# Turning three of the second layer's gelu chunks by DMA transposes instead of on TensorE, and multiplying them by the scan's state one unit later

## The chip, the core and the metric

One core of a Trainium2 chip runs the whole kernel. The metric is the time of one execution in microseconds (us). Before the change three runs gave 3112.25 us as their median, from 3112.09 to 3113.0.

## The reference, cut to what matters

The kernel computes three transformer-like blocks in a row on 256 tokens with 2048 features, in float32. The change lies in the second layer of the first block, the mixer with a recurrence:

```python
def rglru_mixer(h, w_in, conv_w, conv_b, gate_w, gate_b, lru_lambda, w_out):
    proj = h @ w_in
    y_branch, x_branch = jnp.split(proj, 2, axis=-1)
    y_branch = jax.nn.gelu(y_branch)
    xc = causal_depthwise_conv(x_branch, conv_w, conv_b)
    ...                                   # gates r, i from xc; a, u from them
    _, hs = lax.associative_scan(combine, (a, u), axis=1)
    return (hs.astype(h.dtype) * y_branch) @ w_out
```

y_branch is 256 tokens by 2048 features. Its 2048 columns are computed in four chunks of 512. A product has the tokens on the partitions; the scan runs along the tokens, so its state hs has the features on the partitions, and so must hs * y_branch, because it is the stationary side of the next product. So each gelu chunk has to be turned (transposed) before it is multiplied by hs.

## The kernel before, in words

**Units and chunks.** Weights are streamed from DRAM in units of 128 x 1024 float32 (512 KB, two tiles of 128 rows by 512 columns). A chunk is 512 output columns: eight units, and 8 x 12 products on TensorE. Each float32 weight is taken apart into a hi part (ScalarE, L701) and a lo part (VectorE, L1437), and TensorE makes three products per tile and token half (L2337 to L2339). The raw ring has six slots, the ring of hi and lo parts five.

**Order by hand.** Each engine has a class (`Sync`, `Scalar`, `Vector`, `Tensor`, `Pool`) and walks through the same model; in `chunk` a loop over j = 0 to 7 holds one conversion of a unit (`conv`) and, at given j, the side work of this chunk and of the chunk before (`prev`). The loop is written out by hand; nothing is planned by costs. ScalarE and VectorE convert unit j + 3 in their step j, so their step j lies some three units ahead of TensorE's unit j. Conversion of unit u into a ring of five needs TensorE to have finished unit u - 5. TensorE does units 0 and 1 first for token half 0 and then for token half 1, and units 6 and 7 likewise; the others for both halves at once.

**Handing a chunk over.** ScalarE reads token half 0 out of PSUM in its step 7, ahead of that step's conversion (`evac`, L732), and half 1 behind the loop. TensorE starts the next chunk only when half 0 is out (`pair_free`), and its half 1 only when half 1 is out. For a gelu chunk ScalarE then squares it (L739), VectorE makes the tanh's argument (L1456), ScalarE the tanh in step 0 of the next chunk (L747), VectorE the product (L1483). This leaves the gelu, with the tokens on the partitions, in `stg`.

**The recurrence beside it.** During the three chunks that follow the first gelu chunk, and during the first chunk of the product with odd_w_out, a quarter of the scan runs with each: VectorE's scans in steps 1 and 2 (L1918); ScalarE's decays in step 4, which wait for the scans (L1136, L1137, L1140); VectorE's ratio in step 5 (L1904), which waits for them; ScalarE's root in step 6 (L1144), which waits for the ratio; VectorE's drive in step 7 (L1912).

**The turn before the change.** TensorE transposes the eight 128 x 128 blocks of `stg` into PSUM (`turn`, L2368) ahead of its unit 4, VectorE multiplies them by `lru_h` in its step 4 (L1511), ScalarE writes the hi part in step 6 (L806), VectorE the lo part in step 6 (L1618). That instruction raises the semaphore split_done, which TensorE waits for ahead of its next turn. In the first chunk of the product with odd_w_out the turn stands ahead of unit 3.

**The other way to turn, used elsewhere in this kernel.** For 42 chunks of the other stages VectorE takes the upper and lower two bytes of `stg` apart into `tmp` (`bytes_part`, L1537, two copies), SyncE issues one DMA transpose of 2-byte elements (L536), and VectorE puts the bytes together again (`bytes_join`, L1553, two copies). Such a pending chunk has the kind "bytes". With width -1 the transposes go back into `stg` (turned_stg) and not into a buffer of their own. A chunk whose prev is of kind "bytes" waits on TensorE, ahead of its first unit, for all of split_done that is counted so far.

Of the kernel before, what the change touches and what calls it, by code (L numbers as in the profile page):

```python
# [31 lines left out]
ALU = mybir.AluOpType  # L32
# [8 lines left out]
CH = 512  # L41
# [217 lines left out]
def build(nc, i, out):  # L259
# [15 lines left out]
    with ExitStack() as ctx:  # L275
# [148 lines left out]
        class Program:  # L424
# [24 lines left out]
            setup = params = chunk = gates = s5_params = glu = final = mix_at = heads_at = prepare = nothing  # L449

            def turn_slot(self, prev, units, kind):
                if prev is None or prev.kind == "flip" or prev.kind == "bytes" and prev.to[0] != "conv":
                    return -1
                if prev.to[0] == "conv":
                    return 3 if prev.kind == "bytes" else 2
                return 4 if prev.kind == "rope" or prev.kind == "gelu" == kind else min(3, units - 2)
# [21 lines left out]
        class Sync(Program):  # L478
# [61 lines left out]
            def chunk(self, kind, w, units=8, width=CH, lead=None, slot=None, prep=None, order=None,  # L540
                      n=0, apart=False, params=False, **_):
                src, t0, col0 = w
                if lead and lead.kind == "post":
                    self.T.add("x_ready", len(TILES))
                cols = slice(col0, col0 + width) if isinstance(col0, int) else bass.ds(col0, width)
                for j in range(units):
                    if self.preloaded:
                        self.preloaded -= 1
                        continue
                    each = UNIT // width  # L550
                    k = each * (order[j] if order else j)
                    tiles = slice(t0 + k, t0 + k + each) if isinstance(t0, int) else bass.ds(t0 + k, each)
                    self.unit(src[:, tiles, cols], width)
                    if j == 1 and self.apart[0] is not None:
                        self.bytes_turn(self.apart[0])
                        if params:
                            self.load_b_raw()
                    if prep is not None:
                        self.prepare(prep, j)
                    if slot is not None:  # L560
                        self.mix_at(slot + j)
                self.apart = self.apart[1], n if apart else None
# [102 lines left out]
        class Scalar(Program):  # L665
# [144 lines left out]
            def chunk(self, kind, w, units=8, width=CH, prev=None, lead=None, to=None, dst=None, n=0, ss=True,  # L810
# [11 lines left out]
                else:  # L822
                    at = self.turn_slot(prev, units, kind)
                    for j in range(units - AHEAD + 1 if tail else units):
                        if j == units - 1 and kind != "flip":
                            if lead:
                                self.root(D)
                                self.eng.wait_ge(sems["rs_ready"], T.add("rs_ready"))
                            self.evac(kind, ps, 0, dst, width)
                        self.conv()  # L830
                        for p, what, at_j in parts:
                            if at_j == j and what == "square":
                                self.part_square(p)
                            if at_j == j and what == "split":
                                self.late_hi(xlead, p, True)
                        if prep is not None:
                            self.prepare(prep, j)
                            if tail and j == 4:
                                self.prepare(prep, 6)
                        if slot is not None:  # L840
                            self.mix_at(slot + j)
                        if slot1 is not None:
                            self.heads_at(slot1 + j)
                        if order and j >= WINDOW_AT:
                            self.split_window(j - WINDOW_AT)
                        if j == (0 if units == 4 else 1) and self.unsquared is not None:
                            self.square_sums(self.unsquared)
                            self.unsquared = None
                        if j == 0 and final and n:
                            self.part_square(n - 1)  # L850
                        if j == (4 if units == 8 else 1) and stage is not None and n < NCH - 1:
                            for k in ((0, 1) if n == 0 else (n + 1,)):
                                name, l = STAGES[stage]
                                self.load_gain(4 * stage + k, i[name][l, k * CH:(k + 1) * CH])
                        if j == 3 and final and n < NCH - 1:
                            for k in ((0, 1) if n == 0 else (n + 1,)):
                                self.load_gain(16 + k, i["final_g_2"][k * CH:(k + 1) * CH])
                        if prev and prev.kind == "bytes":
                            if j == 3:
                                if prev.width >= 0:  # L860
                                    self.bytes_hi(prev)
                                elif prev.to[0] == "conv":
                                    self.bytes_conv(prev)
                                else:
                                    T.add("split_done")
                                self.stg_till = T.at("split_done")
                        elif j == at:
                            self.split(prev.to)
                        if j == 0 and prev and prev.kind == "flip":
                            self.flip_read(prev)  # L870
                        if j == 3 and prev and prev.kind == "flip":
                            self.flip_hi(prev)
                        if prev and (prev.to[0], j) in (("conv", at + 3), ("lru", at + 2)):
                            self.split_conv(prev.to)
                        if j == 0 and prev and prev.kind == "gelu":
                            self.gelu_finish()
                        if j == 2 and constant:
                            self.lru_constant()
                        if j in (1, 2) and gate is not None:
                            self.gate(gate, j - 1)  # L880
                        if j == 4 and lru is not None:
                            self.lru_decay(lru)
                        if j == 6 and lru is not None:
                            self.lru_root(lru)
# [523 lines left out]
        class Vector(Program):  # L1408
# [93 lines left out]
            def split(self, to):  # L1502
# [4 lines left out]
                    return self.conv_tap(to[1], 0, turn_ps)  # L1507
                if to[0] == "lru":
                    self.eng.wait_ge(sems["turned"], T.at("turned"))
                    self.eng.wait_ge(sems["lru_scanned"], to[1] // 4 + 1)  # L1510
                    nc.vector.tensor_tensor(conv_o[:], turn_ps[:], lru_h[:, to[1]:to[1] + 4], ALU.mult  # L1511
                                            ).then_inc(sems["lru_z"], 1)
                    T.add("lru_z")
                    T.add("split_done")
                    return
                if to[0] in ("plain", "halves"):
                    T.add("split_done")
# [4 lines left out]
                else:  # L1522
                    self.eng.wait_ge(sems["split_hi"], T.add("split_hi"))
                    a = nc.vector.tensor_tensor(to[1], turn_ps[:], to[0].bitcast(F32), ALU.subtract)
                a.then_inc(sems["split_done"], 1)
                T.add("split_done")

            def bytes_part(self):
# [12 lines left out]
            def bytes_join(self, prev):  # L1541
# [5 lines left out]
                if own:  # L1547
                    to = stg[:].rearrange("p m n -> p (m n)").rearrange("p (k s) -> p k s", k=4)
                else:
                    to = joined if prev.to[0] == "conv" else prev.to[1]  # L1550
                to = to.bitcast(U16).rearrange("p k (m t two) -> p m k t two", m=M, two=2)
                for half in range(2):
                    a = nc.vector.tensor_copy(to[:, :, :, :, half],  # L1553
                                              src[:, 8 * half:8 * half + 8].rearrange("p (m k) t -> p m k t", m=M))
                told = "joined" if own or prev.to[0] == "conv" else "split_done"
                a.then_inc(sems[told], 1)
                T.add(told)

# [62 lines left out]
            def chunk(self, kind, w, units=8, width=CH, prev=None, lead=None, to=None, dst=None, n=0, ss=True,  # L1621
# [11 lines left out]
                else:  # L1633
                    at = self.turn_slot(prev, units, kind)
                    for j in range(units - AHEAD + 1 if tail else units):
# [17 lines left out]
                        if j == (0 if units == 4 else 3) and stage is not None and n:  # L1653
                            self.apply_gain(n - 1)
                        if prev and prev.kind == "bytes":
                            if j == 0:
                                self.bytes_part()
                            if j == 3:
                                self.bytes_join(prev)
                            if j == 4 and prev.width >= 0:  # L1660
                                self.bytes_lo(prev)
                            if j == 3 and prev.to[0] == "conv":
# [8 lines left out]
                            self.split_conv(prev.to)  # L1671
                        if prev and prev.to[0] == "lru" and j in (1, 2):
                            self.lru_scan(prev.to[1] // 4, j - 1)
                        if j == 0 and prev and prev.kind == "gelu":
                            self.gelu_finish()
                        if j == 2 and constant:
                            self.lru_constant()
# [1434 lines left out]
        def model(e):  # L3112
# [31 lines left out]
                if c:  # L3144
                    e.gates(c - 1)
            for c in range(4):
                prev = e.chunk("gelu", (w_odd_in, 0, c * CH), x=XT, prev=prev, to=("lru", 4 * c),
                               gate=c + 2 if c < 2 else None, lru=c)
                if c == 0:
                    e.gates(3)  # L3150
# [89 lines left out]
```

## Time and profile before

| | us |
|---|---|
| three runs, median | 3112.25 |
| the profiled execution | 3112.18 |
| its span in the trace | 3110.4 |
| PE busy | 3097.9 (100%) |
| DVE busy | 1989.5 (64%) |
| ACT busy | 1557.4 (50%) |
| POOL busy | 265.6 (9%) |

PE is TensorE's products, PEld its weight loads, DVE is VectorE, ACT ScalarE, POOL GpSimd. The profiled execution lies 0.07 us from the median of the runs, and 1.78 us of it lie outside the span. A busy PE in this table means that its products overlap without a gap; a matmul of 512 columns is shown with some 0.39 us, and the next one starts 0.23 us after it.

### The profile page before, as it was taken

How to read it: one execution, taken by the hardware profiler on the slowest of the kernel's cores; microseconds unless marked ns; L12 is line 12 of the kernel's file. 1: busy time of each engine (PE TensorE's matmuls, PEld its weight loads, DVE VectorE, ACT ScalarE, POOL GpSimd, SP SyncE). 2: the span in 40 equal slices, each digit the busy share in tenths (PEclk: the TensorE clock that was granted, in tenths of full speed). 3: DMA queues.
4: the chain of work that ended last, by engine and by line, in shares of the span. 5: the costliest groups of instructions: out<-in, count | busy, mean ns of one | idle time of the engine just before them, and what ended most of it. 6: DMA issues, size and time to landing. Idle time of an engine off the chain costs nothing.

```text
span 3110.4 us, 37341 instructions
## 1 busy us (share of the span) xinstructions
PE 3097.9 (100%) x14652; PEld 2570.7 (83%) x14652; DVE 1989.5 (64%) x2290; ACT 1557.4 (50%) x2157; POOL 265.6 (9%) x330
## 2 busy tenths in 40 slices
PE   9999999999999999999999999999999999999999
PEld 8788888888888888888888888888888888888887
DVE  6787765656565768676665655668885555555455
ACT  6666543434444669554443434564455443444344
POOL 0000000000000020011820007820000000000000
PEclk9999999999999999999999999999999999999999
DMA  7655676767667556666675766767655766666674
GB/s 246 169 163 172 189 220 193 217 199 205 208 201 225 171 181 190 212 195 212 195 221 184 221 200 223 250 219 228 198 156 176 213 201 202 200 200 209 190 210 155
DMA packets 416944, 623.64 MB, mean 201 GB/s; under 512 B 121169, under 2 KB 132865, under 8 KB 416769
## 3 DMA queue, kind: packets, MB, share of 16 engines
q1 hardware_dynamic: 411376, 614.62, 64.3%
q10 hardware_dynamic: 5392, 6.64, 0.7%
q8 instruction: 116, 1.90, 0.2%
q14 instruction: 60, 0.48, 0.0%
HBM read 587.09 MB, written 11.01 MB: 192 GB/s over the span
## 4 chain that ended last, share of the span: by engine, by line
PE 95%; DVE 2%; ACT 2%; issue 1%; DMA 0%; SPq 0%; ACTq 0%
PE pair L2337 31%; PE pair L2339 30%; PE pair L2338 30%; DVE lo L1437 1%; PE turn_ps L2368 1%; ACT hi L701 0%; PE pair L2768 0%; PE misc_ps L2674 0%; DVE xt_hl L1795 0%; DMA raw<-in_even_w_in 0%; PE misc_ps L2688 0%; DMA turned_bytes<-tmp 0%; PE pair L2657 0%; PE pair L2659 0%; PE pair L2658 0%
## 5 line engine op out<-in xcount | busy, mean ns | idle before, releaser
L1437 DVE TENSOR_TENSOR lo<-raw,hi 128x1024 fp32r<-128x1024 f32 x1084 | 1337.9, 1247 | 711.5 <-ACT hi L701 699.0
L701 ACT ACTIVATE hi<-raw 128x1024 fp32r<-128x1024 f32 x1084 | 1128.9, 1057 | 867.7 <-PE pair L2339 855.5
L2337 PE MATMUL pair<-hi,xt_hl 128*128 128x512 f32 (+1 forms) x2780 | 1089.6, 392 | 2.6 <-DVE lo L1437 1.3
L2339 PE MATMUL pair<-lo,xt_hl 128*128 128x512 f32 (+1 forms) x2780 | 1079.5, 388 | 0.0
L2338 PE MATMUL pair<-hi,xt_hl 128*128 128x512 f32 (+1 forms) x2780 | 1078.8, 388 | 0.0
L2337 PEld LDWEIGHTS pair<-hi,xt_hl 128*128 128x128 f32 x2780 | 522.1, 188 | 114.5 <-issue 2.5
L2339 PEld LDWEIGHTS pair<-lo,xt_hl 128*128 128x128 f32 x2780 | 521.9, 188 | 108.7
L2338 PEld LDWEIGHTS pair<-hi,xt_hl 128*128 128x128 f32 x2780 | 522.4, 188 | 103.6
L2337 PE MATMUL pair<-hi,ht_h 128*128 128x512 f32 x1504 | 586.4, 390 | 0.1
L2339 PE MATMUL pair<-lo,ht_h 128*128 128x512 f32 x1504 | 585.2, 389 | 0.0
L2338 PE MATMUL pair<-hi,ht_l 128*128 128x512 f32 x1504 | 585.2, 389 | 0.0
L2337 PEld LDWEIGHTS pair<-hi,ht_h 128*128 128x128 f32 x1504 | 282.3, 188 | 58.8 <-DVE ht_l L1563 0.5
L2339 PEld LDWEIGHTS pair<-lo,ht_h 128*128 128x128 f32 x1504 | 282.3, 188 | 58.5
L2338 PEld LDWEIGHTS pair<-hi,ht_l 128*128 128x128 f32 x1504 | 282.4, 188 | 58.3
L921 ACT ACTIVATE ht_h<-stg 128x1024 fp32r<-128x1024 f32 x38 | 40.3, 1061 | 157.4 <-DVE stg L1553 157.4
L732 ACT ACTIVATE stg<-pair 128x512 f32<-128x512 f32 x64 | 38.3, 598 | 149.8 <-PE pair L2339 149.1
L2872 POOL TENSOR_TENSOR lru_h<-ht_h,ht_l 128x1024 f32<-128x1024 f32 x4 | 9.8, 2438 | 1164.7 <-ACT gate_i L1120 1164.7
L732 ACT ACTIVATE stg<-pair,stat 128x512 f32<-128x512 f32 x62 | 42.5, 685 | 95.4 <-PE pair L2339 94.9
L1553 DVE COPY stg<-turned_bytes 128x1024 uint16<-128x1024 uint16 x76 | 53.7, 762 | 52.7 <-DMA turned_bytes<-tmp 52.5
L1473 DVE SCALAR_TENSOR_TENSOR acc<-pair,stat,acc 128x512 f32<-128x512 f32 x48 | 36.0, 750 | 75.2 <-PE pair L2339 75.2
L1477 DVE TENSOR_TENSOR xres<-pair,xres 128x512 f32<-128x512 f32 x39 | 26.9, 690 | 55.4 <-PE pair L2339 55.4
L1537 DVE COPY tmp<-stg 128x1024 uint16<-128x1024 uint16 x84 | 54.4, 690 | 0.0
(344 smaller groups left out, 1700.0 us busy)
## 6 DMA issues: line engine op xcount, KB each, us to landing
raw<-in_mlp_w SPq DMA_DIRECT2D x512, 512.0 KB, 4.4
raw<-in_w_gate SPq DMA_DIRECT2D x88, 512.0 KB, 4.4
raw<-in_w_up SPq DMA_DIRECT2D x88, 512.0 KB, 4.0
raw<-in_w_down SPq DMA_DIRECT2D x88, 512.0 KB, 4.4
raw<-in_even_w_in SPq DMA_DIRECT2D x68, 512.0 KB, 4.4
raw<-in_odd_w_in SPq DMA_DIRECT2D x64, 512.0 KB, 4.0
raw<-in_w_in SPq DMA_DIRECT2D x64, 512.0 KB, 4.6
raw<-in_even_w_out SPq DMA_DIRECT2D x32, 512.0 KB, 4.1
```

The source lines that it names most:

```text
L701: nc.scalar.activation(hi[:, r], raw[:, slot], ACT.Copy).then_inc(sems["hi_ready"], 1)
L732: a = nc.scalar.activation(to, ps[:, m, 0:width], func, scale=scale)
L921: nc.scalar.activation(prev.to[0], stg[:].rearrange("p m (f s) -> p (m f) s", s=SEQ), ACT.Copy).then_inc(sems["split_hi"], 1)
L1437: nc.vector.tensor_tensor(lo[:, r], raw[:, slot], hi[:, r].bitcast(F32), ALU.subtract).then_inc(sems["lo_ready"], 1)
L1473: a = nc.vector.scalar_tensor_tensor(dst[:, m], ps[:, m], st(RS2 + m), dst[:, m], ALU.mult, ALU.add)
L1477: a = nc.vector.tensor_tensor(dst[:, m], ps[:, m], dst[:, m], ALU.add)
L1537: a = nc.vector.tensor_copy(planes[:, half], halves[:, half])
L1553: a = nc.vector.tensor_copy(to[:, :, :, :, half], src[:, 8 * half:8 * half + 8].rearrange("p (m k) t -> p m k t", m=M))
L2337: nc.tensor.matmul(to, xh[:, t0 + k, tok], h[:, k], start=s, stop=False)
L2338: nc.tensor.matmul(to, xl[:, t0 + k, tok], h[:, k], start=False, stop=False)
L2339: mm = nc.tensor.matmul(to, xh[:, t0 + k, tok], l[:, k], start=False, stop=e)
L2368: a = nc.tensor.transpose(turn_ps[:, k, m * P:(m + 1) * P], stg[:, m, k * P:(k + 1) * P], ident[:])
```

## The change

The first three gelu chunks get `apart`, so they are handed on as "bytes", with n = -3. In the chunk behind such a one:

- VectorE: the bytes are taken apart in step 1 (ahead of the scans of that step), put together in `tmp` in step 5, and multiplied by the scan's state right behind it, in step 5, ahead of the ratio. The lo part moves from step 6 to step 7.
- SyncE issues the DMA transpose behind unit 2 of its chunk, from `tmp` into `stg`.
- ScalarE waits in step 6 for the joined bytes, ahead of the root; the hi part moves from step 6 to step 7, behind the evacuation of half 0 and that step's conversion.
- TensorE: eight transposes less; the count of split_done goes up ahead of unit 4 without a turn.

The fourth gelu chunk is turned on TensorE as before.

```diff
             def turn_slot(self, prev, units, kind):
-                if prev is None or prev.kind == "flip" or prev.kind == "bytes" and prev.to[0] != "conv":
+                if prev is None or prev.kind == "flip" or prev.kind == "bytes" and prev.to[0] not in ("conv", "lru"):
                     return -1
+                if prev.kind == "bytes" and prev.to[0] == "lru":
+                    return 5
@@ Sync.chunk
-                    if j == 1 and self.apart[0] is not None:
+                    if self.apart[0] is not None and j == (2 if self.apart[0] == -3 else 1):
                         self.bytes_turn(self.apart[0])
@@ Scalar.chunk
                         if prev and prev.kind == "bytes":
-                            if j == 3:
+                            if j == (6 if prev.to[0] == "lru" else 3):
...
+                                elif prev.to[0] == "lru":
+                                    T.add("split_done")
+                                    self.eng.wait_ge(sems["joined"], T.add("joined"))
@@ Vector
+            def lru_z(self, t0, src):
+                T = self.T
+                self.eng.wait_ge(sems["lru_scanned"], t0 // 4 + 1)
+                self.eng.wait_ge(sems["joined"], T.at("joined"))
+                nc.vector.tensor_tensor(conv_o[:], src, lru_h[:, t0:t0 + 4], ALU.mult).then_inc(sems["lru_z"], 1)
+                T.add("lru_z")
+                T.add("split_done")
...
                         if prev and prev.kind == "bytes":
-                            if j == 0:
+                            if j == (prev.to[0] == "lru"):
                                 self.bytes_part()
-                            if j == 3:
+                            if j == (5 if prev.width < -1 else 3):
                                 self.bytes_join(prev)
+                            if j == 5 and prev.to[0] == "lru":
+                                self.lru_z(prev.to[1], joined)
@@ model
             for c in range(4):
-                prev = e.chunk("gelu", (w_odd_in, 0, c * CH), x=XT, prev=prev, to=("lru", 4 * c),
+                prev = e.chunk("gelu", (w_odd_in, 0, c * CH), x=XT, prev=prev, to=("lru", 4 * c), n=-3, apart=c < 3,
                                gate=c + 2 if c < 2 else None, lru=c)
```

In ScalarE's and VectorE's loops the moved steps stand at `at + 2`, with `at` from turn_slot: 4 + 2 before, 5 + 2 after.

## Rows read from the trace of the kernel before

**Rows 1.** The page: busy time by engine, and the chain that ended last.

```profile
PE 3097.9 (100%) x14652; PEld 2570.7 (83%) x14652; DVE 1989.5 (64%) x2290; ACT 1557.4 (50%) x2157; POOL 265.6 (9%) x330
...
PE 95%; DVE 2%; ACT 2%; issue 1%; DMA 0%; SPq 0%; ACTq 0%
```

**Rows 2.** The stretch of the second gelu chunk: busy us by engine, clock, DMA.

```profile
core 0: us, PE busy (x) PEld busy (x) DVE busy (x) ACT busy (x) POOL busy (x), PEclk, DMA share, GB/s
...
1170.00:1197.00 27.00, 27.00 (x141) 22.90 (x139) 25.10 (x20) 26.82 (x37) 5.19 (x2) 1.00 0.61 194
```

**Rows 3.** Timeline of PE, second gelu chunk: start, us, engine, line, operation, count.

```profile
1179.70 0.39 PE L2337 MATMUL pair<-hi,xt_hl 128*128 128x512 f32 x1
...
1185.14 1.03 PE L2368 MATMUL turn_ps<-ident,stg 128*128 128x128 f32 x8
1185.93 0.48 PE L2337 MATMUL pair<-hi,xt_hl 128*128 128x512 f32 x1
1186.25 0.40 PE L2338 MATMUL pair<-hi,xt_hl 128*128 128x512 f32 x1
```

**Rows 4.** The chain that ended last, 1188 to 1198 us: start, us, what.

```profile
1191.14 1.99 ACT hi L701 x2
1193.13 0.94 ACT ht_h L806
...
1195.39 1.16 ACT lru_s L1144
1196.55 0.58 ACT stg L732
1197.17 0.50 PE pair L2337
```

**Rows 5.** Timeline of ACT, third gelu chunk; in brackets idle time before and its releaser.

```profile
1208.97 0.51 ACT L1136 ACTIVATE lru_a<-gate_r,c_lru 128x256 f32<-128x256 f32 x1 [2.12 <-DVE lru_h L1918]
...
1213.28 1.99 ACT L701 ACTIVATE hi<-raw 128x1024 fp32r<-128x1024 f32 x2
1215.17 1.04 ACT L806 ACTIVATE ht_h<-conv_o 128x1024 fp32r<-128x1024 f32 x1
...
1218.59 0.67 ACT L732 ACTIVATE stg<-pair,stat 128x512 f32<-128x512 f32 x1
...
1240.84 0.67 ACT L732 ACTIVATE stg<-pair,stat 128x512 f32<-128x512 f32 x1
```

**Rows 6.** Timeline of DVE, the same chunk.

```profile
1205.37 1.27 DVE L1918 TENSOR_TENSOR_SCAN lru_h<-lru_a,lru_s 128x256 f32<-128x256 f32 x2
...
1211.11 1.22 DVE L1511 TENSOR_TENSOR conv_o<-turn_ps,lru_h 128x1024 f32<-128x1024 f32 x1
1214.36 1.22 DVE L1437 TENSOR_TENSOR lo<-raw,hi 128x1024 fp32r<-128x1024 f32 x1 [2.03 <-ACT hi L701]
1215.50 1.22 DVE L1904 SCALAR_TENSOR_TENSOR lru_s<-lru_s,gate_r 128x1024 f32<-128x1024 f32 x1
```

**Rows 7.** Timeline of DVE, a chunk of the first MLP that is turned by DMA.

```profile
362.34 1.29 DVE L1537 COPY tmp<-stg 128x1024 uint16<-128x1024 uint16 x2
363.55 3.71 DVE L1437 TENSOR_TENSOR lo<-raw,hi 128x1024 fp32r<-128x1024 f32 x3
369.27 1.39 DVE L1553 COPY stg<-turned_bytes 128x1024 uint16<-128x1024 uint16 x2 [2.02 <-DMA turned_bytes<-tmp]
```

**Rows 8.** DMA issues by line: kind, count, median us from issue to landing.

```profile
turned_bytes<-tmp SPq DMA_TRANSPOSE x38, 5.0
...
stg<-tmp SPq DMA_TRANSPOSE x4, 3.8
```

**Rows 9.** Timeline of PE: its last product.

```profile
3102.69 0.39 PE L2339 MATMUL pair<-lo,ht_h 128*128 128x512 f32 x1
```

**Rows 10.** Stretches at the end of the span (columns of rows 2).

```profile
3107.50:3108.00 0.50, 0.00 (x0) 0.00 (x0) 0.00 (x0) 0.00 (x0) 0.00 (x0) 0.99 1.04 401
3108.00:3108.50 0.50, 0.00 (x0) 0.00 (x0) 0.00 (x0) 0.00 (x0) 0.00 (x0) 0.50 1.04 397
```

More of the change, by code:

```diff
@@ L863, in chunk @@
                                     self.bytes_conv(prev)
+                                elif prev.to[0] == "lru":
+                                    T.add("split_done")
+                                    self.eng.wait_ge(sems["joined"], T.add("joined"))
                                 else:
                                     T.add("split_done")
-                                self.stg_till = T.at("split_done")
+                                if prev.to[0] != "lru":
+                                    self.stg_till = T.at("split_done")
                         elif j == at:
@@ L874, in chunk @@
                             self.split_conv(prev.to)
-                        if j == 0 and prev and prev.kind == "gelu":
+                        if j == 0 and prev and (prev.kind == "gelu" or prev.kind == "bytes" and prev.to[0] == "lru"):
                             self.gelu_finish()
@@ L1509, in split @@
                     self.eng.wait_ge(sems["turned"], T.at("turned"))
[L1510 to L1514, printed above, removed]
+                    self.lru_z(to[1], turn_ps[:])
                     return
@@ L1549, in bytes_join @@
                 else:
-                    to = joined if prev.to[0] == "conv" else prev.to[1]
+                    to = joined if prev.to[0] in ("conv", "lru") else prev.to[1]
                 to = to.bitcast(U16).rearrange("p k (m t two) -> p m k t two", m=M, two=2)
@@ L1554, in bytes_join @@
                                               src[:, 8 * half:8 * half + 8].rearrange("p (m k) t -> p m k t", m=M))
-                told = "joined" if own or prev.to[0] == "conv" else "split_done"
+                told = "joined" if own or prev.to[0] in ("conv", "lru") else "split_done"
                 a.then_inc(sems[told], 1)
@@ L1673, in chunk @@
                             self.lru_scan(prev.to[1] // 4, j - 1)
-                        if j == 0 and prev and prev.kind == "gelu":
+                        if j == 0 and prev and (prev.kind == "gelu" or prev.kind == "bytes" and prev.to[0] == "lru"):
                             self.gelu_finish()
```

## The prediction, written before the result was known

> **What bounds the kernel now.** I read the page's busy table and chain first [rows 1]: TensorE is busy for 3097.9 of 3110.4 us and holds 95% of the chain. So what is taken off TensorE shortens the kernel, and what makes it wait lengthens it; work of other engines costs nothing until then. The averages of 64% and 50% for VectorE and ScalarE don't hold in the stage of the change: in the 27 us of the second gelu chunk ScalarE is busy for 26.82 and VectorE for 25.10 [rows 2]. The third view, the chain cut to this place [rows 4], is the one that decides: it doesn't run over TensorE there but over ScalarE: conversions, the hi part (L806), the root (L1144), the evacuation (L732), and only then TensorE's next chunk at 1197.17. TensorE ends the chunk before at 1185.14 + 0.88 + 48 x 0.2267 = 1196.9 (the two figures are worked out in the next part, [rows 3]), so it already starts 0.27 us late. Every us put into this chain shows in the time.
>
> I call the gelu chunks G0 to G3 and the first chunk of the product with odd_w_out W0. The side work of G0 runs beside G1, that of G1 beside G2, and so on. By "evac" I mean ScalarE's evacuation of token half 0, in its step 7.
>
> **What goes.** From the start of the eight transposes to the first product behind them 0.79 us pass, and that product is followed after 0.32 instead of 0.23 [rows 3]: a turn costs 0.88 us. Three turns: -2.64. The 24 products between 1179.70 and 1185.14 give 0.2267 each [rows 3], so a chunk without a turn takes 96 x 0.2267 = 21.76 us on TensorE.
>
> **What comes in, on VectorE.** Taking the bytes apart holds it for 363.55 - 362.34 = 1.21 us, joining them for some 1.4 [rows 7]. The first stands in step 1 ahead of that step's scans, so the scans end 1.2 us later. ScalarE's decays wait for these scans, with 2.12 us of idle time in front of them [rows 5], so they start 1.2 later as well, and so does all that follows. The join comes in step 5, behind a conversion that itself waits for ScalarE (2.03 us [rows 6]). Before, the product with the state (L1511) was done in step 4, inside that waiting time and thus free; now it stands behind the join, ahead of the ratio (L1904), for which ScalarE's root waits.
>
> The lengthening of the stretch from ScalarE's conversion of step 5 to its evac: before it is 1218.59 - 1213.28 = 5.31 [rows 5]. Now: ScalarE's conversion till VectorE's starts 1.12, that 1.14 (1214.36 to 1215.50 [rows 6]), join 1.5 with the semaphore behind it, product 1.13, ratio 1.21, root 1.16 less 0.1 of overlap (its start to the evac's [rows 4]), 0.07 of signal: 7.23. That is +1.92. The moved hi part (L806) leaves this stretch, where it hides nothing any more, and comes behind the evac.
>
> **What comes in, on TensorE.** A chunk whose prev is "bytes" waits ahead of its first unit for all split_done so far. For G2 and G3 that includes the lo part of the chunk before (L1618), now in step 7: evac 0.57, conversion 0.97, hi part 1.04, signal, VectorE behind its own conversion, lo part 1.22: 4.1 us from the start of evac to TensorE's start. Before, only the evac counted (0.6).
>
> **The sum, step by step.** G1: TensorE would be done at 1196.9 - 0.88 = 1196.0. ScalarE's conversion of step 5 stays at 1191.14 [rows 4], because behind the gate work of this chunk the decays didn't wait for the scans; evac at 1191.14 + 7.23 = 1198.4; G2 starts at 1198.4 + 4.1 = 1202.5. Stall 6.5.
> G2: a period from evac to evac was 1240.84 - 1218.59 = 22.25 [rows 5]. Now it grows by 1.24 (bytes apart, ahead of the scans), 1.92 (above) and 0.97 to 1.0 (hi part between the evacuations of half 0 and half 1, from which the next gelu hangs; in its old place it was beside the chain): 26.4 us. Evac at 1224.8, G3 could start at 1228.9; TensorE is done with G2 at 1202.5 + 21.8 = 1224.3. Stall 4.6.
> G3: evac at 1224.8 + 26.4 = 1251.2. W0 isn't preceded by a "bytes" chunk and waits for the evac only, until 1251.9; TensorE done at 1250.6. Stall 1.3.
> W0: its units 6 and 7 need G3's lo part, which hangs from the evac of G3; the turn is back. Against TensorE the chain is 1.1 us later than before, where it had 0.4 to spare, and the hi part of G2's work costs it 0.5 more: stall 1.3.
> Stalls 6.5 + 4.6 + 1.3 + 1.3 = 13.7, less 0.27 of the stall that stands there now, less 2.64: +10.8 us. The same laying-out of steps over the kernel before gives the evacs 1218.61 and 1240.82, where the rows have 1218.59 and 1240.84 [rows 5], so the arithmetic of the chain is good to a tenth; the risk lies in the order that I read from the code.
>
> **What is moved and costs nothing.** SyncE: three transposes, each behind unit 2's load. It waits there for the bytes to be apart; behind it stand only loads of units five and more ahead, some 13 us of cover. Issue to landing took 3.8 us into `stg` (4 of them) and 5.0 into buffers of their own (38) [rows 8]. From the bytes apart to the join there are 10 us in G2 and 12 in G1: hidden. If landing took over 10 us, the rest would come onto the period; 12 us give +14.7 in all. The nearest rows have joins that waited 2.02 us when only three conversions lay between [rows 7]. ScalarE's wait for the join in step 6 ends before the ratio does, so it adds nothing. Copies bounded from both sides: join 1.39 [rows 7] to 2 us, each 0.1 us more shows three times. Nothing is gained by the moves but the transposes.
>
> **The clock.** All of this stage is granted full speed. After its last product, which starts at 3102.69 and ends at 3103.08, TensorE idles and the clock falls from 2.4 to 1.2 GHz at 3108.0, 4.9 us later [rows 9, 10]. The first stall of 6.5 us is longer than that, the second of 4.6 (3.1 if the first units of G2 are slow) isn't. I take it that the clock falls once. How long it stays low no row shows; bounds: nothing lost, and the first two units of G2 at half speed, 5.4 us lost. I take 2.5. Of a loss in G2 the first 1.5 us are hidden, for TensorE waits at the end of G2 for the chain anyway; but then the ring holds the conversions of G2 back. It leaves +1.0. Sum: +11.8.
> The Trainium skill ("TensorE: Matmul & The Clock Gate", section "HAM oscillation — how this bites in real kernels") says that an idle TensorE falls back to half rate, and that the work behind each such gap then starts cold, again and again. By that page the gap at G3 could be paid as well, which is a rival below; the end of this trace agrees with the rule as far as one fall goes.
>
> **Forecast.** The profiled execution took 3112.18 and stands 0.07 from the median. 3112.2 + 11.8 = 3124.0 us. Its own range, with join and signals 0.2 us off per chunk and the clock from 0 to 2.5: 3121 to 3127.
>
> **Rivals.**
> *Hidden after all (slower no more).* VectorE and ScalarE work ahead of TensorE, and the rings of five and six could swallow the delay. The place is evac against the end of TensorE's chunk, the price is 2.64 us gained: 3109.6. It decides if evac comes at most 21.2 us after TensorE's start. For it: TensorE's busy share of 100% in the table. Against it: that margin is used up already [rows 4], and 4.25 us go into each period. 7%.
> *Only the first stall counts*: what is late in G2 and G3 is caught up, since ScalarE's wait of 2.12 and VectorE's of 2.03 [rows 5, 6] shrink. -2.64 + 6.5 = +3.9: 3116.1. Against it: these waits are for one another, not spare. 6%.
> *The clock falls at both gaps and stays low for long* (two units at half speed behind each): +14.7 with one, +18.7 with both: 3127 to 3131. For it: rows 10; against it: the second gap is short. 6%.
> *The change gains* (the turns go and a wait in front of W0 goes too): under 3106 nothing in the rows would give. 1%.
>
> **How the numbers follow.** Forecast 80%, hidden 7, first stall only 6, clock 6, gain 1. A difference of 0.2% (6.2 us) is about what a measurement of this kernel can tell from none. Slower by more: 80 + 6 = 86%; within: 7 + 6 = 13%; faster: 1%. The range from 3117 to 3130 leaves out the first rival, the second by 1 us and the end of the third.
>
> **What would show it.** In the trace after: 24 transposes fewer at L2368; gaps on PE of some 6.5, 4.6 and 1.3 us at the starts of G2, G3 and W0, the first two released by VectorE's lo part and the third by ScalarE's evac; evac to evac 26.4 us instead of 22.25; the joins not waiting for the DMA; a granted clock under 1.00 in G2's first us. I am wrong if evac stays within 21.2 us of TensorE's start, if TensorE's start of G2 isn't released by the lo part, or if the joins wait for the transposes.

## The result, and the profile after

The changed kernel takes 3128.22 us (median of six runs, 3127.32 to 3129.1); the kernel before took 3112.28 in six. The ratio is 1.0051 with an interval of 1.004 to 1.0061: slower by 15.9 us. 3124.0 was forecast, with a range of 3117 to 3130. The time lies inside that range, but above the forecast's own 3121 to 3127, and inside the 3127 to 3131 of the rival in which the clock falls at both gaps; the part on why the prediction was right takes this up.

The page of the kernel after: busy time, the costliest products with what ended the idle time before them, and the transposes by line.

```profile
PE 3100.7 (99%) x14628; PEld 2571.2 (82%) x14628; DVE 1997.1 (64%) x2302; ACT 1557.3 (50%) x2157; POOL 265.6 (8%) x330
...
L2350 PE MATMUL pair<-hi,xt_hl 128*128 128x512 f32 (+1 forms) x2780 | 1091.6, 393 | 14.3 <-DVE ht_l L1629 11.9
...
L2381 PE MATMUL turn_ps<-ident,stg x148: 270/272/273, 39.1 to 3062.4; 128*128 128x128 f32 x148
```

24 transposes are gone (172 to 148), and TensorE is not less busy but more, by 2.8 us [rows 1]: the products run longer at a lower clock. The new idle time lies in front of products that wait for the lo part (L1629, which was L1618 before). Line numbers in this section are those of the changed kernel from here on; each experiment has those of its own kernel, a few lines off.

The timeline of PE: last product of G1 and first of G2, last of G2 and first of G3, first of W0, and W0's first one of units 6 and 7. Then PE's waits between 1170 and 1290 us (total, times, longest).

```profile
1196.16 0.39 PE L2352 MATMUL pair<-lo,xt_hl 128*128 128x512 f32 x1
1204.11 0.79 PE L2350 MATMUL pair<-hi,xt_hl 128*128 128x512 f32 x1 [7.56 <-DVE ht_l L1629]
...
1227.23 0.39 PE L2352 MATMUL pair<-lo,xt_hl 128*128 128x512 f32 x1
1231.92 0.79 PE L2350 MATMUL pair<-hi,xt_hl 128*128 128x512 f32 x1 [4.30 <-DVE ht_l L1629]
...
1257.75 0.50 PE L2350 MATMUL pair<-hi,ht_h 128*128 128x512 f32 x1 [0.95 <-ACT stg L734]
...
1276.17 0.50 PE L2350 MATMUL pair<-hi,ht_h 128*128 128x512 f32 x1 [0.89 <-DVE ht_l L1629]
```

```profile
PE pair L2350 <- DVE ht_l L1629: 12.7, 3, 7.6
...
PE pair L2350 <- ACT stg L734: 1.0, 1, 1.0
```

These are the stalls at G2, G3 and W0 with the releasers that were forecast; the third wait for the lo part (0.89) is W0's, ahead of its units 6 and 7, and was forecast too. Before the change G2 started at 1197.17 [rows 4]. A product that starts at 1227.23 frees its place 0.23 us later, so the true stalls are some 7.7, 4.5, 1.1 and 1.0 us.

The timeline of ACT in the kernel after, side work of G1 beside it, and the evacuations of the next two chunks:

```profile
1191.56 1.99 ACT L703 ACTIVATE hi<-raw 128x1024 fp32r<-128x1024 f32 x2
1197.70 1.28 ACT L1150 ACT_TABLE_LOAD   x1 [4.15 <-DVE lru_s L1917]
1198.99 1.15 ACT L1150 ACTIVATE lru_s<-lru_s,stat 128x1024 f32<-128x1024 f32 x1
1200.05 0.67 ACT L734 ACTIVATE stg<-pair,stat 128x512 f32<-128x512 f32 x1
1200.62 1.04 ACT L703 ACTIVATE hi<-raw 128x1024 fp32r<-128x1024 f32 x1
1201.56 1.04 ACT L808 ACTIVATE ht_h<-conv_o 128x1024 fp32r<-128x1024 f32 x1
...
1227.86 0.67 ACT L734 ACTIVATE stg<-pair,stat 128x512 f32<-128x512 f32 x1
...
1257.02 0.67 ACT L734 ACTIVATE stg<-pair,stat 128x512 f32<-128x512 f32 x1
```

And DVE in the same kernel and place:

```profile
1192.64 1.23 DVE L1443 TENSOR_TENSOR lo<-raw,hi 128x1024 fp32r<-128x1024 f32 x1 [1.03 <-ACT hi L703]
1193.78 1.38 DVE L1564 COPY tmp<-stg 128x1024 uint16<-128x1024 uint16 x2
1195.26 1.22 DVE L1535 TENSOR_TENSOR conv_o<-tmp,lru_h 128x1024 f32<-128x1024 f32 x1
1196.41 1.22 DVE L1917 SCALAR_TENSOR_TENSOR lru_s<-lru_s,gate_r 128x1024 f32<-128x1024 f32 x1
...
1201.69 1.22 DVE L1443 TENSOR_TENSOR lo<-raw,hi 128x1024 fp32r<-128x1024 f32 x1 [2.94 <-ACT hi L703]
1202.84 1.22 DVE L1629 SCALAR_TENSOR_TENSOR ht_l<-conv_o,ht_h 128x1024 fp32r<-128x1024 f32 x1
```

The same load in the kernel before, beside G2, and all four of these loads in the kernel after (busy time, mean ns, idle time before them):

```profile
1216.24 1.28 ACT L1144 ACT_TABLE_LOAD   x1
```

```profile
L1150 ACT ACT_TABLE_LOAD x4 | 5.1, 1283 | 12.5 <-DVE lru_s L1917 12.4
```

Read them together. The join (1193.78) has no bracket, so it does not wait for the DMA. From ScalarE's conversion of step 5 (1191.56) to its evac (1200.05) 8.49 us pass, where 5.31 passed before [rows 5]; I had 7.23. The missing 1.26 is in the second line of ACT's timeline: ScalarE's table load for the root, 1.28 us, starts only when the ratio is done (1197.63), so it lies on the chain. Before the change it started at 1216.24, ahead of the end of its ratio at 1216.72 [rows 6], and with no idle time in front of it. Of the four loads in the kernel after, three have 4.15, 4.15 and 4.14 us of idle time in front, together all of the 12.4; the fourth, beside W0, has no wait for a join ahead of it and does not wait. From evac to evac it is 27.81 us and then 29.16, where it was 22.25 [rows 5]. TensorE's start at 1204.11 follows 4.06 us behind the evac, as worked out (4.1).

The clock of the kernel after in the two gaps and behind them (columns of rows 2):

```profile
1200.00:1200.50 0.50, 0.00 (x0) 0.00 (x0) 0.00 (x0) 0.50 (x2) 0.00 (x0) 0.88 0.90 131
1200.50:1201.00 0.50, 0.00 (x0) 0.00 (x0) 0.00 (x0) 0.50 (x2) 0.00 (x0) 0.50 0.69 262
...
1230.50:1231.00 0.50, 0.00 (x0) 0.00 (x0) 0.50 (x2) 0.50 (x1) 0.00 (x0) 1.00 0.00 0
1231.00:1231.50 0.50, 0.00 (x0) 0.00 (x0) 0.50 (x1) 0.47 (x1) 0.00 (x0) 0.59 0.00 0
...
1231.50:1237.50 6.00, 5.58 (x13) 4.42 (x14) 5.84 (x6) 4.82 (x5) 0.00 (x0) 0.50 0.45 132
```

It fell from 2.4 to 1.2 GHz in both gaps, 3.8 and 3.5 us after the last product had ended. G2 took 1227.46 - 1204.11 = 23.35 us instead of 21.76, so 1.6 were lost; G3, measured in the same way, some 24.7, so 3.0.

The first evacuation of W0's product by DVE closes the stage, before and after:

```profile
1262.83 0.69 DVE L1475 COPY acc<-pair 128x512 f32<-128x512 f32 x1 [2.19 <-PE pair L2339]
```

```profile
1279.22 0.69 DVE L1481 COPY acc<-pair 128x512 f32<-128x512 f32 x1 [1.97 <-PE pair L2352]
```

It comes 16.39 us later, 0.42 of which are there already when the stage begins (ScalarE's 1191.14 [rows 4] against 1191.56). So 15.97 us of the 16.8 between the two spans lie in this stage; the profiled execution took 3129.1 us, 0.9 more than the median. TensorE's own account of the stage closes: stalls of 7.7 + 4.5 + 1.1 + 1.0, clock losses of 1.6 + 3.0, less the 0.3 of stall that stood there before, less 2.6 for the turns, make 16.0.

### The profile page after: what moved, and what is told of

The parts are those of the page before. It is cut to its first block, busy times and chain, and to the rows that moved or that the text cites. A ratio compares the mean times of both kernels' runs of the same rounds, so it can differ in the third digit from the quotient of the medians.

```text
span 3127.2 us, 37314 instructions
## 1 busy us (share of the span) xinstructions
PE 3100.7 (99%) x14628; PEld 2571.2 (82%) x14628; DVE 1997.1 (64%) x2302; ACT 1557.3 (50%) x2157; POOL 265.6 (8%) x330
## 4 chain that ended last, share of the span: by engine, by line
PE 57%; DVE 1%; ACT 1%; issue 0%; DVEq 0%; ACTq 0%
PE pair L2350 19%; PE pair L2352 18%; PE pair L2351 18%; DVE lo L1443 1%; PE pair L2781 0%; PE turn_ps L2381 0%; ACT hi L703 0%; PE misc_ps L2797 0%; DVE xt_hl L1808 0%; PE turn_ps L2840 0%; PE misc_ps L2802 0%; PE pair L2734 0%; DVE xres L1834 0%; DVE glu_z L2216 0%; PE misc_ps L2816 0%
## 5 line engine op out<-in xcount | busy, mean ns | idle before, releaser
L2350 PEld LDWEIGHTS pair<-hi,xt_hl 128*128 128x128 f32 x2780 | 523.2, 188 | 127.3 <-DVE ht_l L1629 12.7
```

The source lines that it names most:

```text
L2350: nc.tensor.matmul(to, xh[:, t0 + k, tok], h[:, k], start=s, stop=False)
```

## The experiments

All are against the kernel before on the same chip. The prediction's +10.8 us for chain and turns, with three table loads of 1.28 added, comes to +14.6; the stage measured 15.97, so some 1.3 are left for the clock. The following runs take links out of the chain, single ones at first.

**e1: the moves alone, without the DMA.** Edit to the kernel before:

```diff
-                return 4 if prev.kind == "rope" or prev.kind == "gelu" == kind else min(3, units - 2)
+                return 5 if prev.kind == "gelu" == kind else 4 if prev.kind == "rope" else min(3, units - 2)
```

> The kernel before with the steps moved and nothing else: the three gelu chunks are still turned on TensorE, now ahead of unit 5, multiplied in VectorE's step 5 ahead of the ratio, hi and lo part in step 7. No bytes, no DMA, no wait ahead of a chunk. Theory (the chain from ScalarE's evacuation to its next one bounds this stage, and every us that is put into it shows): product 1.14 ahead of the ratio, hi part 0.97 between the two evacuations, less what the hi part freed: period 23.6 us instead of 22.25, stalls of some 0.6, 1.0, 1.0 and 1.3 us, in all +3.8 us, 3116.1. Rival (only the bytes' copies, the wait ahead of the chunk and the clock cost anything): within 1 us of before, 3112 to 3113.

Measured: 3114.98 us against 3112.21, +2.8 (ratio 1.001, 1.0001 to 1.002). Evacs at

```profile
1196.74 0.66 ACT L732 ACTIVATE stg<-pair,stat 128x512 f32<-128x512 f32 x1
...
1220.17 0.66 ACT L732 ACTIVATE stg<-pair,stat 128x512 f32<-128x512 f32 x1
...
1243.59 0.67 ACT L732 ACTIVATE stg<-pair,stat 128x512 f32<-128x512 f32 x1
```

so 23.4 us apart, and TensorE waited for three of them (1.3 us in all) and once for the lo part (0.9). The same transposes, one step later and ahead of the ratio, already cost 2.8 us. The rival, that only bytes, wait and clock cost anything, falls. The forecast was 1 us too high.

**e2: ScalarE's wait for the join moved behind the root.** Edit to the changed kernel:

```diff
@@ Scalar.chunk, step 6
                                     T.add("split_done")
-                                    self.eng.wait_ge(sems["joined"], T.add("joined"))
@@ ahead of the evacuation
+                        if j == units - 1 and prev and prev.kind == "bytes" and prev.to[0] == "lru":
+                            self.eng.wait_ge(sems["joined"], T.add("joined"))
                         if j == units - 1 and kind != "flip":
```

> The changed kernel with ScalarE's wait for the joined bytes moved from step 6 (ahead of the root) to step 7 (ahead of the evacuation). Theory: with two waits in front of the root its table load of 1.28 us comes behind both; with one it is done while ScalarE waits, as before the change. Evac to evac 26.5 instead of 27.8 in the third gelu chunk, TensorE starts G2 at 1202.5 to 1202.9 instead of 1204.1; in all +11 us over before instead of +16, 3123 to 3124. Rival (the table load waits for the ratio's data whatever stands ahead of it): no difference, 3128.

Measured: 3124.56 us against 3112.21, +12.4 (1.0041, 1.0026 to 1.0056): 3.6 less than the changed kernel, where three loads of 1.28 are 3.84, and 0.6 above the forecast's upper end of 3124. ACT's timeline in e2:

```profile
1192.99 1.28 ACT L1151 ACT_TABLE_LOAD   x1
1197.09 1.15 ACT L1151 ACTIVATE lru_s<-lru_s,stat 128x1024 f32<-128x1024 f32 x1 [2.81 <-DVE lru_s L1918]
1198.14 0.67 ACT L734 ACTIVATE stg<-pair,stat 128x512 f32<-128x512 f32 x1
```

The load is back ahead of the wait, and the evac comes 7.16 us behind the conversion at 1190.98, where 7.23 had been worked out before the result. So it is the second wait that put the load behind. The clock fell at both gaps in e2 too: the second gap, 2.97 us long, cost TensorE some 1.7 us, which the forecast doesn't name. The Trainium skill ("Perfetto Trace Analysis", section "Identifying Dependency Chains") says that an instruction that waits for several engines may get semaphore instructions of their own ahead of it. That is near this case but not it, since both waits here are for VectorE (the join and the ratio); how the two waits were laid out as instructions no view here shows.

**e3: no wait ahead of G2 and G3.** Edit to the changed kernel:

```diff
-                if prev and prev.kind == "bytes":
+                if prev and prev.kind == "bytes" and prev.to[0] != "lru":
                     self.eng.wait_ge(sems["split_done"], T.at("split_done"))
+                if prev and prev.kind == "gelu" and kind == "set":
+                    self.eng.wait_ge(sems["split_done"], T.at("split_done", 1))
```

> The changed kernel without TensorE's wait for split_done ahead of G2 and G3 (they don't read what it guards); W0 waits for it instead. Theory (the chain of ScalarE and VectorE is the bound, the wait only moves the stalls): evac to evac stays near 27.7, stalls of 4.3, 4.3 to 5.9 and 4.3 to 5.9 us at G2, G3 and W0 instead of 7.6, 4.3 and 1.0, in all +14.6 over before, 3127, the 1.5 us less than the changed kernel being the clock's. Rival (the wait is the cause): only evac is late, the stalls ahead of G2 and G3 shrink by 3.4 us each, 3121.

Measured: 3127.83 us against 3112.21, +15.6 (1.005, 1.0035 to 1.0065). PE's timeline in e3, the starts of G2, G3 and W0:

```profile
1200.40 0.79 PE L2350 MATMUL pair<-hi,xt_hl 128*128 128x512 f32 x1 [4.21 <-ACT stg L734]
...
1227.87 0.50 PE L2350 MATMUL pair<-hi,xt_hl 128*128 128x512 f32 x1 [2.82 <-ACT stg L734]
...
1255.39 0.76 PE L2350 MATMUL pair<-hi,ht_h 128*128 128x512 f32 x1 [5.42 <-issue]
```

This is the run that says most. The wait that the trace of the changed kernel names for 12.7 us is gone, and 0.4 us come back. TensorE starts G2 3.7 us earlier and loses that further on: it waits 5.4 us ahead of W0, where it waited 0.95 and 0.89. The trace names no releaser for this last wait, and the edit puts a wait for split_done there; but W0 starts 0.77 us behind the evac at 1254.62, as it did in the changed kernel (0.73), so it is the evac that holds it and not the moved wait. The period (evacs at 1199.68, 1227.15 and 1254.62, 27.47 apart) is set by ScalarE and VectorE.

**e4: filler products in the gaps.** Edit to the changed kernel, ahead of the wait for split_done at G2 and G3; the products go to turn_ps and are not read:

```diff
+                if prev and prev.kind == "bytes" and prev.to[0] == "lru" and prev.to[1] >= 4:
+                    self.fill(24 if prev.to[1] == 4 else 16)
```

> The changed kernel with 24 products ahead of TensorE's wait at G2 and 16 ahead of that at G3, written to the free turn_ps and not read: the clock stays at full speed, and 2 to 2.5 us of each wait are left. It measures what the clock costs. Theory: evac of G3 comes 1.5 us earlier, since the conversions that wait for the first slow units of G3 aren't late: +14.6 over before, 3126.7. Rival (each us at half speed shows in full, 1.6 in G2 and 2.9 in G3): 4.5 less, 3123.7. Other rival (nothing): 3128.2.

Measured: 3127.22 us against 3112.21, +15.0 (1.0049, 1.0034 to 1.0064). At G3 the clock stayed at 1.00, and the period up to G3's evac is 1254.83 - 1227.35 = 27.48 instead of 29.16: 1.7 us of the 3.0 lost in G3 had shown. At G2 it fell all the same (below), so this run takes away only one of the two falls. It is 1.0 us faster than the changed kernel by the medians, and 1.5 by the stage in the two traces; the rest of what the clock took from TensorE is hidden in its waits for the chain.

**e5: the ratio ahead of the join.** Of e2, and in VectorE's step 5:

```diff
+                        if j == 5 and prev and prev.kind == "bytes" and prev.to[0] == "lru":
+                            self.lru_ratio(lru)
                         if prev and prev.kind == "bytes":
...
-                        if j == 5 and lru is not None:
+                        if j == 5 and lru is not None and not (prev.kind == "bytes" and prev.to[0] == "lru"):
                             self.lru_ratio(lru)
```

> Of e2 (join wait in step 7), and VectorE's ratio ahead of the join and the product in step 5. Theory: what stands between ScalarE's conversion of step 5 and its evac shrinks by 2.6 us of join and product, so evac of G1 comes at 1196.4 as in the kernel before; the period stays 24.5 us, by the bytes taken apart ahead of the scans (1.24) and the hi part between the evacuations (0.97). The wait for split_done is the only large one left: stalls of 4.6, 2.8 and 0.6 us, in all +5.2 over before, 3117.4. If the clock falls in the first gap, up to 1 us more. Rival (the join and the product themselves are too much for VectorE in this stage, wherever they stand): 3122 and more, as e2.

Measured: 3119.67 us against 3112.35, +7.3 (1.0024, 1.0015 to 1.0033), from 3118.13 to 3123.01. It takes 4.9 us less than e2, so join and product cost by their place, not by being there. It is 2.1 us over the forecast, and 1.1 over that with a fallen clock. PE and ACT in e5:

```profile
1201.08 0.80 PE L2353 MATMUL pair<-hi,xt_hl 128*128 128x512 f32 x1 [4.50 <-DVE ht_l L1630]
```

```profile
1196.33 0.69 ACT L734 ACTIVATE stg<-pair,stat 128x512 f32<-128x512 f32 x1 [0.16 <-DVE tmp L1565]
...
1223.30 0.69 ACT L734 ACTIVATE stg<-pair,stat 128x512 f32<-128x512 f32 x1 [1.02 <-PE pair L2355]
```

The first gap is the forecast one (4.6); the one at G3 is shorter, 1.5 instead of 2.8. The clock fell behind the first, and G2 took 24.7 us on TensorE. With the chain shorter, TensorE is late enough that the evac of G2 waits for it (1.02 us) and comes 26.97 us behind the evac of G1 instead of the 24.5 of the forecast. So here most of the 2.9 us lost show, where e4 found them half hidden.

**e6: e5, without the wait ahead of G2 and G3, and the bytes taken apart behind the scans.** The edit of e3 is in it, and SyncE's transpose stands behind unit 3; VectorE's part:

```diff
-                            if j == (prev.to[0] == "lru"):
+                            if j == 0 and prev.to[0] != "lru":
                                 self.bytes_part()
...
                             self.lru_scan(prev.to[1] // 4, j - 1)
+                            if j == 2 and prev.kind == "bytes":
+                                self.bytes_part()
```

> Of e5, and besides no wait for split_done ahead of G2 and G3 (as e3), and the bytes taken apart behind the scans of step 2 instead of ahead of those of step 1 (SyncE's transpose one unit later). Theory: period 23.3 us; stalls of 0.7, 1.2, 1.2 and 1.3 us and some 0.3 at unit 1 of each chunk, in all +2.7 over before, 3114.9: each of the two is worth what it puts into the chain. Rival (the chain isn't it, but the stalls at the starts of chunks, so without the wait the transposes' 2.6 us are gained): 3110.

Measured: 3114.97 us against 3112.35, +2.6 (1.0008, 0.9999 to 1.0017). As the theory has it (2.7); the rival's 3110 is missed by 5 us. Evacs come at 1196.38, 1219.44 and 1242.50, 23.06 apart (23.3 forecast). Two things were changed at once, so the run doesn't show what each is worth by itself.

**e7: e6, with the hi and the lo part of the products that are made beside G1 and G2 in steps 2 and 3 of the next chunk.** In ScalarE's loop (VectorE's alike, with step 3 and without the wait):

```diff
-                            self.split_conv(prev.to)
+                            if prev.kind == "bytes" and prev.to[0] == "lru" and prev.to[1] < 8:
+                                self.owed = prev.to
+                                self.eng.wait_ge(sems["lru_z"], T.at("lru_z", -1))
+                            else:
+                                self.split_conv(prev.to)
+                        if j == 2 and self.owed:
+                            self.split_conv(self.owed)
+                            self.owed = None
```

> Of e6, and the hi and the lo part of G1's and G2's products in steps 2 and 3 of the chunk behind, where ScalarE waits for TensorE. Theory: period 22.1 us as before the change, in all +0.4 over before, 3112.6: even with all put aside the transposes' 2.64 us are not gained, because ScalarE's and VectorE's chain of 22.1 us, not TensorE's 21.8, sets the period, and W0 waits 1.3 us for its last part. Rival (TensorE's time is what counts once the stalls are gone): 3109.6 to 3110.5.

Measured: 3112.64 us against 3112.35, +0.3 (1.0001, 0.9992 to 1.0011). Evacs at 1195.87, 1217.82 and 1239.75, 21.9 apart. Two waits are left on TensorE, 0.58 us for the lo part of a conversion in G1 (1191.17) and 0.99 for G3's lo part ahead of W0's units 6 and 7. The period is only 0.2 us over TensorE's 21.76, and the evac of G3 comes 1.09 us earlier than in the kernel before (1239.75 against 1240.84, 0.14 of it there when the stage begins); W0's wait gives that back. TensorE has 2.64 us less to do, and the two other engines don't let it gain by that.

**e8: only the first gelu chunk by DMA.** Edit to the changed kernel: `apart=c == 0`.

> The changed kernel with only the first of the gelu chunks turned by DMA (side work beside G1), the other two on TensorE as before. Theory: evac of G1 at 1199.7; G2's prev isn't of kind bytes, so TensorE waits for the evac alone: 4.3 us ahead of G2, 0.6 ahead of G3, nothing at W0, less one turn of 0.88: +3.8 over before, 3116.1, up to 3117.1 if the clock falls. Rival (each such chunk costs the same third of the loss): +5.3, 3117.6.

Measured: 3117.13 us against 3112.35, +4.8 (1.0015, 1.0005 to 1.0025), from 3116.4 to 3118.1. The gap at G2 is 4.21 us, released by the evac, and the clock falls behind it. This is the forecast with a fallen clock (3117.1) and near the rival's 3117.6, so by its time alone the run doesn't part the two. What speaks for the theory is the releaser and the length of the gap, and that TensorE waits nowhere else in the stage.

**e9 and e10: the ratio ahead of step 5's conversion,** in e7 and in the kernel before:

```diff
                             self.evac(kind, ps, 0, dst, width)
+                        if j == 5 and lru is not None:
+                            self.lru_ratio(lru)
                         self.conv()
```

> Of e7, and VectorE's ratio ahead of that step's conversion instead of behind it, so that ScalarE's root doesn't wait for a conversion of ScalarE, then of VectorE, then the ratio. Theory: the period of ScalarE and VectorE falls from 22.1 to 21.2 us, under TensorE's 21.8; only then can the turns' 2.64 us be gained, less 0.36 for W0's last part: 2.3 under before, 3110.0. Rival (W0's wait or something later gives it back): 3112.

> The kernel before with VectorE's ratio ahead of step 5's conversion, and nothing else. Theory: ScalarE's chain gets shorter, but TensorE with its turns (22.6 us a chunk) is the bound there; only the 0.27 us ahead of G2 can go: 0.1 to 0.3 under before, 3112.1. Rival (what e9 gains is the early ratio and not the turns): as much as e9.

Measured: e9 3110.86 us (3110.21 to 3112.33, 11 runs) against 3112.37 (21 runs), -1.5; the ratio 0.9996 has an interval of 0.9987 to 1.0005, so a gain is likely but not shown. e10 3112.23 (0.9999, 0.999 to 1.0008). ACT's evacs of G2 and G3 and DVE's first of W0 in e9:

```profile
1217.07 0.67 ACT L736 ACTIVATE stg<-pair,stat 128x512 f32<-128x512 f32 x1
...
1238.56 0.67 ACT L736 ACTIVATE stg<-pair,stat 128x512 f32<-128x512 f32 x1
```

```profile
1260.75 0.69 DVE L1491 COPY acc<-pair 128x512 f32<-128x512 f32 x1 [1.97 <-PE pair L2370]
```

The period is 21.5 us, under TensorE's 21.76, and the stage closes 2.08 us earlier than before; 0.46 of that is there already when it begins (evac of G0 at 1168.43 against 1168.89), so the stage itself gives 1.6 us of the forecast's 2.3. The early ratio in the kernel before brings nothing that can be told: there TensorE is the bound with its turns.

## Why the prediction was right, and where it was short

- *The chain through ScalarE bounds this stage.* Right for the changed kernel, and shown: e3 takes away the wait that the trace names and gets 0.4 us back, e2, e5, e6 and e7 shorten the chain and get back about what they take out. In the kernel before the chain was only close to the bound: a chunk with its turn takes TensorE 22.6 us, the period was 22.25, and e10 shortens the chain and gains nothing that can be told.
- *The turns give 2.64 us.* Right as a term of TensorE's time, but it is given back as a wait in every variant until the chain is under 21.8 us (e9; in e7 the period is 21.9 and nothing is gained).
- *Stalls of 6.5, 4.6, 1.3 and 1.3 us.* Measured 7.7, 4.5, 1.1 and 1.0. Place, order and releasers as forecast.
- *"ScalarE's wait for the join in step 6 ends before the ratio does, so it adds nothing."* This step failed. The wait ends before, and still puts the root's table load of 1.28 us behind the ratio, three times: 3.84 us of the 4.1 by which the forecast was short. The load stands nowhere in the sum of 7.23 us from conversion to evac; 8.49 were measured. e2 shows it.
- *The clock falls once, behind the 6.5 us gap; 2.5 us lost, 1.0 of it showing.* It fell twice: the second fall came 3.5 us after a product's end, where the only row before the result had 4.9 [rows 9, 10], and I took a shorter gap for safe. Lost were 1.6 and 3.0 us. Of the second 1.7 showed, by e4 (29.16 - 27.48); of the first at most 0.3 (27.81 against the 27.47 of e3). The Trainium skill's rule ("TensorE: Matmul & The Clock Gate", section "HAM oscillation — how this bites in real kernels") of a cold start behind each such gap holds here at both.
- *The rival in which the clock falls at both gaps, 3127 to 3131.* The measured 3128.22 lies in its range, and the clock did fall twice. But the rival had 5.4 us lost behind each gap, where 1.6 and 3.0 were; its time comes out because the table load, which it doesn't have, stands in for the rest. It was right in the two falls and by luck in the time.
- *The bytes' copies, the DMA and the join.* Right: 1.21 and 1.4 us, nothing waited for the transposes.
- *From evac to TensorE's start 4.1 us.* Measured 4.06.
- *The sum.* +10.8 for chain and turns becomes 14.6 with the table load, against 15.97 in the stage. The 1.3 between them agree with what e4 gives for the clock. That 3128 lies inside 3117 to 3130 it owes to the width of that range, which was made for other doubts; none of them was a table load.

## What to carry to other kernels

When the engine that is busy for 100% is fed by a chain over other engines, look at the stage and at what starts its next block before taking work off it: here TensorE had 0.4 us a chunk to give (22.6 against a period of 22.25) and 0.9 were taken off it, at the price of 5.6 us more of chain. The wait that a trace names for most of the idle time need not be the bound: follow the period of the engines behind it. And put a new wait where nothing that could run ahead of it, such as a table load, stands behind it.

## What the runs showed of the hardware that was not expected

- In this kernel a second wait in front of the root, which needs another table, moved the table load (1.28 us) behind both waits: 1197.70 with two, 1192.99 with one (e2).
- The clock's fall after TensorE's last product had ended: 4.9 us at the end of the kernel before, 3.8 and 3.5 in the changed kernel, 2.9 ahead of G2 in e2 and 3.0 ahead of G2 in e3. It also fell with products already running again. In e4 the filler ended at 1201.4, the products began at 1203.44 after 2.08 us, and the clock fell at 1203.7:

```profile
1195.77 5.60 PE L2362 MATMUL turn_ps<-xt_hl 128*128 128x512 f32 x24
...
1203.44 0.59 PE L2350 MATMUL pair<-hi,xt_hl 128*128 128x512 f32 x1 [2.08 <-DVE ht_l L1629]
```

```profile
1203.50:1204.00 0.50, 0.50 (x2) 0.41 (x3) 0.50 (x1) 0.50 (x2) 0.00 (x0) 0.72 1.01 184
1204.00:1204.50 0.50, 0.50 (x3) 0.41 (x2) 0.50 (x2) 0.50 (x1) 0.00 (x0) 0.50 0.73 266
```

In e2 it fell 0.8 us after the products had begun again behind a gap of 2.97 us (1228.89). The same lengths also left it at 1.00: a gap of 2.08 us ahead of W0 in e4, one of 2.82 ahead of G3 in e3, one of 0.68 at G3 in e4. So the length of one gap does not decide it here, and what does is open.
